# SSD rounds with the chunk step first on VectorE and the weight subtraction in halves; last stages on 516 and 512 token columns in place of 528

## What is computed

```
h = concatenate([zeros(PAD), meta(16), x(512)])
z, xbc, dt_raw, q, k, v, g_ssd, g_att = split_cols(rmsnorm(h) @ w_in, IN_WIDTHS)
xbc = silu(causal_dwconv(xbc, conv_w, conv_b))        # 4 taps
y = ssd_chunked(x, dt, a, B, C) + d_skip * x          # chunks of 128 tokens
y_ssd = gated_group_rmsnorm(y, z, ssd_norm_w) @ w_ssd_branch
y_att = swa_sink_attention(q, k, v, ...) @ w_attn_branch
merged = sigmoid(g_ssd + b0) * y_ssd + sigmoid(g_att + b1) * y_att
h = h + merged @ w_out
hid = causal_dwconv(rmsnorm(h) @ w_ffn_in, ffn_conv_w, ffn_conv_b)   # 3 taps: a token and the two before it
up, gate = split(hid)
h = h + (silu(gate) * up) @ w_ffn_out
return rmsnorm(h)[:, BLOCK:]                          # the 512 real tokens
```

## Time and profile before

| | |
|---|---|
| median of 3 runs | 2574.65 us (2573.96 to 2580.72) |
| profiled execution: time, span | 2573.06 us, 2571.2 us |
| TensorE matmuls busy | 2451.2 us (95%), 15333 |
| TensorE weight loads busy | 2180.7 us (85%) |
| VectorE busy | 1554.3 us (60%) |
| ScalarE busy | 881.5 us (34%) |
| GpSimd busy | 62.3 us (2%) |
| DMA | 242.49 MB, 94 GB/s mean |
| mean granted TensorE clock | 0.977 of full |

### The profile page before, as it was taken

One profiled execution on the slowest core, in us unless ns is written; L12 is line 12 of the kernel. 1 busy time (PEld: TensorE's weight loads), 2 busy tenths in 40 slices (PEclk: granted clock), 3 DMA queues, 4 the chain that ended last, 5 costly groups with the idle time before them and its releaser, 6 DMA issues.

```text
span 2571.2 us, 39857 instructions
## 1 busy us (share of the span) xinstructions
PE 2451.2 (95%) x15333; PEld 2180.7 (85%) x15333; DVE 1554.3 (60%) x2793; ACT 881.5 (34%) x1347; POOL 62.3 (2%) x55
## 2 busy tenths in 40 slices
PE   7999999999988999999999989998998999999997
PEld 4887888888887888888878879888998899999997
DVE  5555444456476755344467876876665655883784
ACT  3123122234254533212245751663332333222122
POOL 0000000000121000000000000000100000000000
PEclk9999999999978899999999999998999999999999
DMA  4236224424432012222224422431211122223222
GB/s 146 84 104 145 95 88 148 129 90 123 160 102 55 21 45 83 97 98 98 82 98 105 109 70 73 112 99 66 96 68 64 65 82 83 98 82 132 82 91 106
DMA packets 91774, 242.49 MB, mean 94 GB/s; under 512 B 24886, under 2 KB 58166, under 8 KB 67638
## 3 DMA queue, kind: packets, MB, share of 16 engines
q1 hardware_dynamic: 29056, 198.26, 22.1%
q10 hardware_dynamic: 60808, 36.42, 6.5%
q0 software_dynamic: 1760, 5.77, 1.0%
HBM read 230.51 MB, written 11.14 MB: 94 GB/s over the span
## 4 chain that ended last, share of the span: by engine, by line
PE 83%; DVE 7%; issue 5%; ACT 3%; DMA 1%; ACTq 1%; DVEq 0%
PE ps L966 40%; PE ps L1201 27%; PE ps L1302 3%; PE ps L1155 3%; PE ps L1100 1%; PE ps L1138 1%; DVE wlo L1462 1%; PE ps L1387 1%; ACT whi L516 1%; PE ps L1361 1%; ACT L L811 1%; DMA buckets<-in_buckets 1%; PE ps L1059 1%; PE ps L1127 1%; ACTq L802 1%
## 5 line engine op out<-in xcount | busy, mean ns | idle before, releaser
L516 ACT ACTIVATE whi<-raw 128x2048 fp32r<-128x2048 f32 x187 | 357.7, 1913 | 737.5 <-PE ps L966 495.8
L1201 PE MATMUL ps<-parts,whi 128*128 128x264 f32 x2752 | 484.9, 294 | 9.2 <-DVE sq L2091 3.7
L1462 DVE TENSOR_TENSOR wlo<-raw,whi 128x2048 fp32r<-128x2048 f32 (+1 forms) x197 | 429.1, 2178 | 65.5 <-ACT whi L516 64.9
L966 PE MATMUL ps<-parts,whi 128*128 128x512 f32 x1360 | 430.3, 398 | 0.0
L1201 PEld LDWEIGHTS ps<-parts,whi 128*128 128x128 f32 x2752 | 392.7, 191 | 21.5 <-issue 15.5
L966 PEld LDWEIGHTS ps<-parts,whi 128*128 128x128 f32 x1360 | 256.3, 189 | 62.2 <-issue 1.6
L966 PE MATMUL ps<-parts,wlo 128*128 128x512 f32 x680 | 269.6, 396 | 0.0
L1201 PE MATMUL ps<-parts,wlo 128*128 128x264 f32 x1200 | 245.3, 286 | 0.0
L966 PE MATMUL ps<-Mhi,whi 128*128 128x512 f32 x512 | 203.0, 396 | 0.0
L966 PE MATMUL ps<-Mlo,whi 128*128 128x512 f32 x512 | 203.0, 396 | 0.0
L966 PE MATMUL ps<-Mhi,wlo 128*128 128x512 f32 x512 | 203.0, 396 | 0.0
(11 more groups left out here) (361 smaller groups left out, 3878.6 us busy)
## 6 DMA issues: line engine op xcount, KB each, us to landing
raw<-in_stream SPq DMA_DIRECT2D x187, 1024.0 KB, 4.8
bands<-scratch ACTq DMA_DIRECT2D x8, 1024.0 KB
csb<-sums_d ACTq DMA_DIRECT2D x16, 512.0 KB, 5.7
near<-bands ACTq DMA_DIRECT2D x20, 256.0 KB, 2.6
csf<-sums_d ACTq DMA_DIRECT2D x32, 128.0 KB, 5.9
Qst<-parts POOLq DMA_DIRECT2D x14, 256.0 KB, 6.1
tabs<-bands ACTq DMA_DIRECT2D x8, 418.0 KB, 4.1
X<-in_x SPq DMA_DIRECT2D x4, 512.0 KB, 16.2
```

What stands on the lines that cost most here:

```text
L516: nc.scalar.activation(whi[:, s, :], raw[:, s, :], ACT.Copy).then_inc(hi_done, 1)
L966: mm = nc.tensor.matmul(out, w[:, s, at], x(k), start=k + j == 0, stop=k == k_tiles - 1 and j == 2)
L1201: mm = nc.tensor.matmul(ps[:, 2 * par + h, 0:HALF], w[:, s, at], x[:, k, h * HALF:(h + 1) * HALF], start=k + j == 0, stop=k == k_tiles - 1 ...
L1462: low = nc.vector.tensor_tensor(wlo[:, s, a:b], raw[:, s, a:b], whi[:, s, a:b].bitcast(F32), ALU.subtract)
```

## The change

On VectorE, chunk rounds run `turned` first, ahead of `evacuate`. The weight subtractions of rounds 8 to 16 are cut in two: columns 0 to 1023 at the end of the even round, columns 1024 to 2047 in the next round, behind `evacuate`. On ScalarE, `decays(0)` of round 6 moves behind that round's silu. The stages att, out and ff_in drop the first 12 of the 16 learned tokens (CUT = 12): `tile2` gets a start column, and its two halves have 258 columns in place of 264; the steps on VectorE and ScalarE between them have 516 columns. The FFN's convolution, its product and its down projection are made for the 512 real tokens alone, and the down projection issues one matmul of 512 columns in place of two of 264.

```diff
+CUT = N_META - 4
+LATE = TOK - CUT
...
+        def late_product(par):
+
+            return ps[:, 2 * par:2 * par + 2, 0:LATE // 2]
...
 (ScalarE, SSD rounds)
-                    if r == TOK_AT + 4:
-                        act.wait_ge(tokh_ready, i + 1)
-                        decays(0)
...
                     if 0 < r <= 12:
                         act.wait_ge(xbc_new, i * 12 + r)
                         nc.scalar.activation(conv_out(r - 1), conv_out(r - 1), ACT.Silu).then_inc(xs_ready, 1)
+                        if r == TOK_AT + 4:
+                            act.wait_ge(tokh_ready, i + 1)
+                            decays(0)
...
 (TensorE, tile2, called with a=CUT for att, out and ff_in)
+                w = (TOK - a) // 2
...
-                            mm = nc.tensor.matmul(ps[:, 2 * par + h, 0:HALF], w[:, s, at], x[:, k, h * HALF:(h + 1) * HALF],
+                            mm = nc.tensor.matmul(ps[:, 2 * par + h, 0:w], wt[:, s, at], x[:, k, a + h * w:a + (h + 1) * w],
...
 (TensorE, down projection)
-                    tile2(f"ff_out{f}", c, 0, (Fhi, Flo), range(b - a), b - a, 1, ready=(lambda k: (f_ready, a + k + 1)) if not c else None)
+                    u, t = U0[f"ff_out{f}"] + c, T0[f"ff_out{f}"] + c
+                    pe.wait_ge(lo_done, u + 1)
+                    pe.wait_ge(mt_free, t - 1)
+                    for k in range(b - a):
+                        if not c:
+                            pe.wait_ge(f_ready, a + k + 1)
+                        at = slice(k * P, (k + 1) * P)
+                        for j, (wt, x) in enumerate(((whi, Fhi), (whi, Flo), (wlo, Fhi))):
+                            mm = nc.tensor.matmul(ps[:, 2 * (t % 2), :], wt[:, u % 2, at], x[:, k, N_META:], start=k + j == 0, stop=k == b - a - 1 and j == 2)
+                    mm.then_inc(mt_full, 1)
...
 (VectorE, SSD rounds)
                 for r in range(21):
+                    if r in SCAN_AT:
+                        turned(*SCAN_AT[r])
                     if r:
                         evacuate(r - 1)
+                    if r % 2 and 8 < r < 18:
+                        split_low("half", r // 2 - 1, i * 14, 1)
...
-                    if r in SCAN_AT:
-                        turned(*SCAN_AT[r])
...
                     if r and r % 2 == 0:
-                        split_low("half", r // 2 - 1, i * 14)
+                        split_low("half", r // 2 - 1, i * 14, 0 if 8 <= r < 18 else None)
...
 (VectorE, last stages; the other steps of att, out and ff_in likewise)
-                            nc.vector.tensor_tensor(halves(Fstg[:, m, 2:]), product(m), halves(R[:, :]), ALU.mult).then_inc(mt_free, 1)
+                            nc.vector.tensor_tensor(halves(Fstg[:, m, :]), late_product(m), halves(R[:, CUT:]), ALU.mult).then_inc(mt_free, 1)
...
-                    x = halves(X[:, k, :])
-                    nc.vector.tensor_tensor(x, x, product(k % 2), ALU.add).then_inc(mt_free, 1)
+                    x = X[:, k, N_META:]
+                    nc.vector.tensor_tensor(x, x, ps[:, 2 * (k % 2), :], ALU.add).then_inc(mt_free, 1)
```

More of the change, by code:

```diff
@@ L912, in _ @@
             for k in range(KT):
[L913 removed]
+                nc.scalar.activation(GA[:, k, CUT:], GA[:, k, CUT:], ACT.Tanh, scale=0.5, bias=gate_h[:, KT + k:KT + k + 1]).then_inc(ga_sig, 1)
             for c in range(4):
@@ L1183, in _, with tile2 @@
             mlp("mlp1", 4, tiles(Nhi, Nlo, N_META), 3)
-            def tile2(layer, c, m, rhs, ks=range(KT), k_tiles=KT, m_tiles=2, turn=0, ready=None, free=None, parity=0):
+            def tile2(layer, c, m, rhs, ks=range(KT), k_tiles=KT, m_tiles=2, turn=0, ready=None, free=None, parity=0, a=0):
+                w = (TOK - a) // 2
                 s, t = (U0[layer] + c) % 2, c * m_tiles + m
@@ L1425, in _ @@
                     for m in range(2):
-                        tile2("att", c, m, A2, ks, ready=(lambda k: (at_ready, k + 1)) if not c + m else None)
+                        tile2("att", c, m, A2, ks, ready=(lambda k: (at_ready, k + 1)) if not c + m else None, a=CUT)
             for c in range(4):
@@ L1429, in _ @@
                     for m in range(2):
-                        tile2("out", c, m, H2, ks, ready=(lambda k: (mg_ready, k + 1)) if not c + m else None)
+                        tile2("out", c, m, H2, ks, ready=(lambda k: (mg_ready, k + 1)) if not c + m else None, a=CUT)
             for f, (a, b) in enumerate(((0, FF_CUT), (FF_CUT, FFT))):
@@ L1436, in pair @@
                                 norm_spread(FF_NORM, True)
-                            tile2(f"ff_in{f}", c, m, A2, ks, turn=turn, ready=(lambda k: (h_ready, KT * 6 + k + 1)) if first and not m else None)
+                            tile2(f"ff_in{f}", c, m, A2, ks, turn=turn, ready=(lambda k: (h_ready, KT * 6 + k + 1)) if first and not m else None, a=CUT)
                         if first and not m:
@@ L2207, in _ @@
                 heads_low(3)
+            own.mark(nc.vector.memset(acc[:, 0:CUT], 0.0))
             own.wait()
@@ L2227, in _ @@
                 dve.wait_ge(mt_full, T0["out"] + k + 1)
-                x = halves(X[:, k, :])
-                nc.vector.scalar_tensor_tensor(x, product(k % 2), 0.5, x, ALU.mult, ALU.add).then_inc(mt_free, 1)
-                norm_tile(FF_NORM, 6, k, k % 2, "norm_ffn", 0, AThi, ATlo)
+                x = halves(X[:, k, CUT:])
+                nc.vector.scalar_tensor_tensor(x, late_product(k % 2), 0.5, x, ALU.mult, ALU.add).then_inc(mt_free, 1)
+                norm_tile(FF_NORM, 6, k, k % 2, "norm_ffn", CUT, AThi, ATlo)
                 if k % 2:
                     split_low("out", k // 2)
-            own.mark(nc.vector.memset(Fstg[:, :, 0:2], 0.0))
             norm_scale(FF_NORM, NC)
@@ L2261, in _ @@
                         up, gate = Fcv[:, 0, :], Fcv[:, 1, :]
-                        nc.vector.tensor_tensor(t_at(Fhi, k), up, gate, ALU.mult).then_inc(f_hi, 1)
+                        nc.vector.tensor_tensor(t_at(Fhi, k, N_META), up, gate, ALU.mult).then_inc(f_hi, 1)
                         own.mark(nc.vector.tensor_tensor(up, up, gate, ALU.mult))
```

28 lines of the change are left out of this document (13 added, 15 removed).

## The result

The changed kernel runs in 2547.95 us (median of 4 runs, 2544.86 to 2551.42) against 2577.54 us for the kernel before in the same sitting (2573.96 to 2580.72): ratio 0.9886, 95% interval 0.9865 to 0.9907. The forecast was 2540.7 us with a range of 2533 to 2555. The profiled execution took 2548.19 us with a span of 2546.3 us, 24.9 us under the span of before, where the prediction's sum has 34.0. The medians differ by 29.6 us, 24.0 to 34.8 by the interval: the profiled execution of before was 4.5 us under its median, that of the changed kernel 0.2 over it.

A forecast was written before the change was run, and what follows sets the result against it. The prediction took TensorE as the bound, with waits on VectorE and ScalarE in the SSD rounds. Terms 9.1 + 12.1 + 7.8 + 5.0 = 34.0 us off 2573.06 gave 2539.1, plus 1.6 for the median: 2540.7 us, range 2533 to 2555.

The forecast's parts named there:

- Silu ahead of decays(0): Round 7, both passes: TensorE's waits behind ScalarE's silu vanish, with the first pass's low clock; 9.1 us saved.
- Chunk first, rounds 13 to 17: VectorE's chunk step comes earlier, so TensorE's waits for the product with L shrink; 6.05 us a pass, 12.1 in two.
- Rounds 8 to 11, nothing: VectorE has no slack; later states cancel the shorter waits for L: zero gain, ends -3.4 and +2.4 us.
- 258 columns: att, out and ff_in: 2880 matmuls six columns narrower save 2.7 ns each, 7.8 us; other end 1.4 us.
- rival (b): att, out, ff_in: 258 columns pace like 264, at a floor; 7.8 us becomes 1.4, total 2547.1 us; chance 0.08.
- Rival (d): att, out, ff_in: halves starting 12 columns into a row leave the fast pace; slower, near 2796 us; chance 0.03.
- One matmul of 512: Down projection: one matmul replaces two of 264 columns, 10.2 ns saved a pair; net 5.0 us.
- (a): Rival: ScalarE bounds rounds 13 to 17, or a state wait uses the gain up; 12.1 us lost, 2552.8; chance 0.21.
- (c): Rival: the low clock vanishes altogether, in round 15 too; 3 us more gained, 2537.7 us; chance 0.08.
- (e): Rival: ScalarE's L holds the product, silu waits for input, columns hit the floor; 5 us or less, 2570; chance 0.03.

The follow-up runs named there:

- the last stages alone: The changed kernel with its SSD-round edits undone, keeping the narrower columns and the one matmul of 512: 2570.76 us, ratio 0.9969 to the kernel before.
- experiment with rounds 8 and 10: The changed kernel with VectorE's evacuation put back ahead of the chunk step in rounds 8 and 10: 2544.26 us, ratio 0.9862 to the kernel before.

## Why the prediction was right or wrong

**Silu ahead of decays(0), 9.1 us: right.** The waits of 3.5 and 3.3 are gone, the first pass's round 7 is 2.4 us shorter (2.3 forecast), 9.2 us; the run with this edit alone shows it by itself. That the low clock cost 2.3 us was read from one execution; with the last stages alone it cost 1.5 us in each pass, 3.0 in all, so the size of this part is partly luck, and its presence is not.

**Chunk first, rounds 13 to 17, 12.1 us: right, nearly wait by wait.** Forecast were waits of 0.9, 3.0 and 0.6 us in rounds 14, 15 and 17, the trace has 0.90, 3.21 and 0.27 (0.49 with the weight loads). The sum is 5.4 + 6.3 = 11.7 us. The low clock of round 15 stayed, as forecast; in the first pass it lasted longer (from the transposes of round 15 to those of 16 it took 15.62 us at a mean clock of 0.78, in the second 14.38 at 0.88). The premise that the gate step of round 13 does not move holds: 10.34 us behind that round's transposes before, 10.35 after.

**Rounds 8 to 11, nothing: right, with the named cause.** Rounds 8 to 10 were reckoned at 32.3 us and take 32.65; rounds 11 and 12 gain the 1.2. Together +0.8 us in both passes. What is late next is the state, as said, but without a low clock behind its waits. Where they would stand was partly wrong: forecast were 1 to 2 us in odd rounds, and there are 0.7 and 0.8 before rounds 9 and 11 and 1.8 before round 10. The experiment with rounds 8 and 10 shows that this price could have been avoided: the prediction had the reason (TensorE's transposes leave a hole which the evacuation formerly filled) and took it as given.

**258 columns, 7.8 us: the term that failed.** The slope of 0.45 ns a column was right and 258 columns do not stand on the floor of rival (b); what the step left out is that the second half starts at byte 1080. It measured 1.5 ns in place of 2.7, 4.2 us over 2880 matmuls, between the two ends that the prediction kept (1.4 and 7.8). Rival (d) had the right suspicion, that halves which begin 12 columns into a row might leave the fast pace, and took its price from a row of another kind (86 ns); a price of 2.4 ns a pair makes nothing slower. Of the gap between 2540.7 and the measured time this is 3.6 us. The Trainium skill, "TensorE: Matmul & The Clock Gate", Back-to-back issue gap, has N / 2.4 + 2.5 ns, by which, as an estimate, 8 columns are 3.3 ns; the runs show 3.6, and the rule has no term for the start, which moves the pace here by up to 2.25 ns at the same N.

**One matmul of 512, 5.0 us: right.** The whole of att to the end is 9.6 us shorter, less 4.2 for the columns: 5.4. A tile of 12 k-tiles takes 58.93 / 7 = 8.42 us (8.4 forecast), and the wait for the last unit's subtraction stands at 2.5 (2.4 before), so the first tile gained nothing, as said.

**What the sum left out: what is given back behind the rounds.** The wait for Gr grew by 1.2 and 0.35 us, the end of the first pass by 1.6, the end of the second by 0.5, and 1.2 us of low clock came in ahead of the rounds: 4.9 us. The prediction followed the gain up to the group sum and no further. The first two are a new wait in the changed kernel that stands in all kernels with both edits of VectorE and the old order at the group sum (3.1 to 3.2 us, against 2.0 to 2.8 in the others). The others hang on where stretches of low clock fall, which differs between the executions; that they belong to the change is not shown. So 34.0 - 0.8 (rounds 8 to 12) - 3.6 (columns) - 0.4 (group 1) + 0.5 (silu 0.1, 512 columns 0.4) - 4.9 = 24.8, and 24.9 was measured between the two spans.

**The time as a whole.** The measured 2547.95 us lies in the range of 2533 to 2555, and 1 us outside the narrower one, 2534 to 2547, that went with the forecast. It is 7.3 us over 2540.7: the sum is 9.1 too high for the two profiled executions, less 1.8 because the changed kernel's profiled execution stood at its median and not 1.6 us under it. By the medians the change is worth 29.6 us with an interval of 24.0 to 34.8, which still holds the 34.0; that the sum is too high rests on the rows, not on the times.

**Rivals.** (a) said that ScalarE bounds rounds 13 to 17 and uses the gain up. The gain was not used up, so it fell as a forecast; but ScalarE's silu of z was indeed what bound these rounds afterwards, and 12.5 us were left there, more than the 11.7 that the change gained. The prediction saw the 4.02 us before the gate step and wrote that it does not move. (c) did not come: round 15 kept its low clock until the silu of z was moved. (e) fell with the first view of the waits.

## What to carry to other kernels

When an engine waits for an instruction that is short and has had its input for long, look at what its own engine does first: twice here a silu of 0.65 us stood behind a decay step of 5 to 7 us that nobody wanted yet, and moving it was worth 9.2 and 12.5 us, two of the three largest terms of the study. A stretch gained ahead of a reduction is only gained when the chain behind it is followed as well, since its waits grow by what they now come early. And when a tile is cut to fewer columns, place the start of every piece as well as its width: a second piece that starts at column 270 and not 272 took back nearly half of the gain.

## What the runs showed of the hardware that was not expected

- The start of the moving operand (the data that stream past the loaded weights) changes the pace of a stream of fp32r matmuls. At 256 columns: 118.1 ns from bytes 64 and 1088 of the row, 120.4 from bytes 56 and 1080. Starts at bytes 0, 48, 1056, 64 and 1088 show no cost, 1080 costs 2.4 to 2.9 ns and 56 costs 1.6 to 2.1. The free ones are multiples of 16 bytes and the dear ones are not; five and two values are too few to call it a rule. Two outputs side by side across the border of two PSUM banks (260 columns at the end of one, 256 at the start of the next) cost nothing (119.0 ns measured, 119.05 by the slope).
- Rounds without low clock repeat to within 0.05 us between kernels that share an order (rounds 8 to 10: 32.63 to 32.67 us in all seven kernels with the chunk step first in each), while whole executions of one kernel differ by 10 us. From round 14 to the group sum, where stretches of low clock fall, the same rounds take 43.87 to 44.90 us in kernels that differ only elsewhere. The differences between whole executions go with the granted clock: of the kernel with rounds 8 and 10 changed, one execution had a span of 2547.0 us at a mean clock of 0.976, another 2537.3 at 0.981. So a comparison between landmarks resolves 0.1 us where the clock stays up and 1 us where it does not; medians of four to seven executions resolve 3 to 5.
